# Weight ring numbered through the sections, second-block token-major evictions on ScalarE, and three moved steps, in a two-block hybrid transformer kernel

## The reference

```python
def first_block(x, c, ...):            # two hybrid_layers, then rms_norm(h, final_g)
    mod = silu(c) @ w_ada + b_ada      # shift, scale, gate
    u = rms_norm(x, g) * (1 + scale) + shift
    z = u @ w_in                       # 18 pieces: q, k, v, gates of three attentions
    merged = (sigmoid(ma) * (ya @ w_br_a) + sigmoid(mb) * (yb @ w_br_b)
              + sigmoid(mc) * (yc @ w_br_c))
    return x + gate * (merged @ w_out)

def second_block(x, c, ctx, c_ctx, ...):   # two mixer_layers
    h  = x  * (1 + scale)   + shift        # latent tokens
    hc = cx * (1 + scale_c) + shift_c      # 256 context tokens
    a_q, a_i, a_ff, a_fb, b_q, b_k, b_v, c_q, c_k, c_v, d_q, d_k, d_v, g = split(h @ w_in)
    # ... and the same pieces of hc @ w_in
    y_a = hgrn2_mixer(...)       # gated scan in both directions, rms-normed per head
    y_b = global_gqa(...)        # latent queries on latent + context keys
    y_c = diff_attention(...)    # softmax(q1 k1) - lam * softmax(q2 k2)
    y_d = window_gqa_latent(...) # window with a sink
    x_new = layer_norm(alpha * x + gate * (concat(y_a..y_d) * silu(g) @ w_out), ln_g, ln_b)
    # the first layer also makes cx_new in the same way; the last does not
```

## Time and profile before

| | |
|---|---|
| median of 3 runs | 1502.31 us (1502.21 to 1502.62) |
| profiled execution, its own time | 1501.21 us |
| span of its instructions | 1499.2 us |
| mean granted TensorE clock | 0.987 |
| TensorE busy | 96% of the span |
| VectorE / ScalarE / GpSimd busy | 37% / 27% / 10% |
| DMA engines, mean share | 40%, 147 GB/s |

### The profile page before, as it was taken

The page is one execution under the profiler, slowest core; times in us unless marked ns, Lnnn a source line. Parts: engine busy times, 40 slices in busy tenths (PEclk is TensorE's granted clock), DMA queues, the critical chain, the costliest instruction groups (busy, mean ns, idle before and its releaser), DMA issues.

```text
span 1499.2 us, 20302 instructions
## 1 busy us (share of the span) xinstructions
PE 1440.3 (96%) x8186; PEld 1169.1 (78%) x8186; DVE 550.4 (37%) x1295; ACT 408.1 (27%) x755; POOL 146.2 (10%) x191
## 2 busy tenths in 40 slices
PE   5999999999999999999999999999999998999986
PEld 3888788888878878888888888876777787877765
DVE  1252212112126332314244422145663631455454
ACT  1112212412021222333312313232342412433332
POOL 0110200000011030000111100012220000142100
PEclk9999999999999999999999999999999999999999
DMA  9544544355445444443333433345315342322200
GB/s 375 219 158 152 202 169 169 144 193 206 159 169 197 168 169 169 150 175 134 123 137 113 140 113 113 140 168 204 129 62 196 113 155 84 141 85 85 85 28 29
DMA packets 31484, 221.95 MB, mean 148 GB/s; under 512 B 3872, under 2 KB 4000, under 8 KB 4896
## 3 DMA queue, kind: packets, MB, share of 16 engines
q1 hardware_dynamic: 31392, 220.67, 40.0%
HBM read 219.60 MB, written 1.05 MB: 147 GB/s over the span
## 4 chain that ended last, share of the span: by engine, by line
PE 90%; DVE 4%; ACT 2%; DMA 1%; issue 1%; POOL 1%; SPq 0%; DVEq 0%; ACTq 0%; POOLq 0%
PE event L869 45%; PE event L860 9%; PE event L1029 6%; PE event L1073 5%; PE logits L961 3%; PE mixed_out L1017 3%; PE event L826 3%; PE turns L980 3%; PE event L1041 2%; PE event L1100 2%; DMA ring<-in_w 1%; PE event L1173 1%; PE event L891 1%; PE event L1054 1%; PE event L848 1%
## 5 line engine op out<-in xcount | busy, mean ns | idle before, releaser
L869 PE MATMUL event<-u,ring 128*128 128x256 f32 x3200 | 718.7, 383 | 12.0 <-DMA ring<-in_w 4.9
L869 PEld LDWEIGHTS event<-u,ring 128*128 128x128 f32 x3200 | 605.4, 191 | 112.8 <-issue 22.7
L860 PE MATMUL event<-ring,u 128*128 128x256 f32 (+1 forms) x704 | 151.0, 371 | 0.0
L860 PEld LDWEIGHTS event<-ring,u 128*128 128x128 f32 x704 | 127.3, 190 | 22.1 <-issue 6.2
L1248 ACT ACTIVATE region<-event 128x512 f32<-128x512 f32 x72 | 43.1, 598 | 292.1 <-PE event L869 291.8
L1284 ACT ACTIVATE S<-logits,stat 128x512 f32<-128x512 f32 (+2 forms) x160 | 84.0, 535 | 130.2 <-DVE stat L1628 125.5
L1976 POOL TENSOR_TENSOR raw<-raw,tables 128x512 f32<-128x512 f32 (+1 forms) x28 | 33.6, 1201 | 772.3 <-PE event L891 464.6
L1073 PE MATMUL event<-region,ring 128*128 128x256 f32 x384 | 85.3, 380 | 2.9 <-DVE region L1771 2.9
L1029 PE MATMUL event<-region,ring 128*128 128x256 f32 x384 | 84.4, 380 | 0.0
L1073 PEld LDWEIGHTS event<-region,ring 128*128 128x128 f32 x384 | 72.2, 190 | 15.7 <-issue 6.4
L1029 PEld LDWEIGHTS event<-region,ring 128*128 128x128 f32 x384 | 72.6, 190 | 11.1 <-issue 1.4
(11 more groups left out here) (206 smaller groups left out, 1318.0 us busy)
## 6 DMA issues: line engine op xcount, KB each, us to landing
ring<-in_w SPq DMA_DIRECT2D x204, 1024.0 KB, 4.8
tables<-in_two SPq DMA_DIRECT2D x1, 1600.0 KB, 9.0
x<-in_x SPq DMA_DIRECT2D x1, 1024.0 KB, 15.1
x<-in_ctx SPq DMA_DIRECT2D x1, 1024.0 KB, 7.0
out<-x SPq DMA_DIRECT2D x4, 256.0 KB, 2.1
tables<-in_one SPq DMA_DIRECT2D x1, 832.0 KB, 10.9
tables<-in_late SPq DMA_DIRECT2D x1, 512.0 KB, 7.0
consts<-in_common SPq DMA_DIRECT2D x1, 320.0 KB, 3.4
```

The costliest lines, as they stand in the source:

```text
L860: ins = mm(bank[:, t * 256:t * 256 + width], mem.u[:, q, k, t * P:(t + 1) * P], wt[:, k * 256:k * 256 + width], start=k == 0, stop=k == KB ...
L869: ins = mm(bank[:, j * 256:(j + 1) * 256], wt[:, k * 256 + j * P:k * 256 + j * P + P], mem.u[:, q, k, :], start=k == 0, stop=k == KB - 1)
```

## The change

1. Ring slots are numbered by the row of the unit in the whole weight array, not in the section. Each used-up unit requests the row five further on, over the ends of sections as well.
2. In the second block's projections ScalarE evicts `vv`, `hi` and `fv` (both the latent's and the context's, in `one1` too). VectorE keeps `av`, `bv`, `cv` of the first block.
3. `feed 1 v1` in `two0` moves from in front of `fv` to behind `hi`.
4. `feed 0 v1` at the end of `two0` moves in front of the second half of `kk 1`, so on ScalarE its biases come ahead of the eviction of `kk 1`.
5. `norm h0` in `two1` moves to the front of its slot, ahead of the second half of `fv 1`.

```diff
-                      proj("fq"), ("rot", "fk", 0), ("mod", "v1"), ("feed", 1, "v1"), proj("fv"), ("rot", "fq", 0), proj("hi"), proj("ff", 1),
+                      proj("fq"), ("rot", "fk", 0), ("mod", "v1"), proj("fv"), ("rot", "fq", 0), proj("hi"), ("feed", 1, "v1"), proj("ff", 1),
...
-    return s + [("mean", 0), ("half", proj("kk", 1)), ("var", 0), proj("kk", 1), ("feed", 0, "v1")]
+    return s + [("mean", 0), ("half", proj("kk", 1)), ("var", 0), ("feed", 0, "v1"), proj("kk", 1)]
...
+    n = next(h for h, items in enumerate(fill) if ("norm", "h0") in items)
+    fill[n].remove(("norm", "h0"))
+    fill[n].insert(0, ("norm", "h0"))
...
-            n = u + RING if u + RING < len(units) else len(units) + u % RING
-            if row + n < ROWS:
+            n = row + u + RING
+            if n < ROWS:
...
-                slot = u % RING
-                eng.dma_start(mem.ring[:, slot, :], dram["w"][row + n]).then_inc(sems[f"landed{slot}"], 16)
+                slot = n % RING
+                eng.dma_start(mem.ring[:, slot, :], dram["w"][n]).then_inc(sems[f"landed{slot}"], 16)
...
-                slot = u % RING
+                row = first_row(sec) + u
+                slot = row % RING
...
-                    eng.wait_ge(sems[f"landed{slot}"], w.at(f"landed{slot}", 16 * (u // RING + 1)))
+                    eng.wait_ge(sems[f"landed{slot}"], 16 * (row // RING + 1))
...
-                if name in ("av", "bv", "cv", "hi", "fv", "vv"):
+                if name in ("av", "bv", "cv"):
                     continue
...
+                if name == "vv":
+                    both = split2(bank)
+                    act(to["gv"], both[:, :, 0:P], func)
+                    act(to["nv"], both[:, :, P:2 * P], func).then_inc(drained[e % BANKS], 1)
+                elif name in ("hi", "fv"):
+                    act(to[name], split2(bank), func).then_inc(drained[e % BANKS], 1)
...
-            elif kind == "proj" and item[1] in ("av", "bv", "cv", "hi", "fv", "vv"):
+            elif kind == "proj" and item[1] in ("av", "bv", "cv"):
```

More of the change, by code:

```diff
@@ L341, in __init__ @@
         events = sum(self.events(i) for i in script)
-        units = sum(map(has_unit, script))
         for b in range(BANKS):
             n[f"full{b}"] = n[f"drained{b}"] = len(range(b, events, BANKS))
-        for s in range(RING):
-            n[f"landed{s}"] = 16 * len(range(s, units, RING))
         for q in ("logits_ready", "exps_done", "probs_ready", "turned", "turns_copied", "mixed", "y_copied"):
@@ L691, in program @@
                      lambda n, s: ctx.enter_context(nc.psum_tensor(n, s, F32)))
-        names = sorted({q for sec in SECTIONS for q in sec.per}) + [
+        names = sorted({q for sec in SECTIONS for q in sec.per}) + [f"landed{s}" for s in range(RING)] + [
             "pe_links", "dve_links", "act_links", "pool_links", "consts_in", "cond_in", "x0_in", "params_in", "rest_in", "tables_in", "stored",
@@ L1233, in body @@
                     func = ACT.Silu
-                if name == "kk" and q == 0:
+                if name == "vv":
[4 more added lines that the diff above has]
+                    act(to[name], split2(bank), func).then_inc(drained[e % BANKS], 1)
+                elif name == "kk" and q == 0:
                     eng.wait_ge(sems["rope_done"], w.at("rope_done", 0))
@@ L1572, in body @@
                     dst, src = mem.one["bv"][:, :, 0:132], src[:, :, 0:132]
-                elif one:
+                else:
                     dst = mem.one[name][:, :, i * 256:(i + 1) * 256]
[L1575 to L1581, removed]
                 eng.tensor_copy(dst, src).then_inc(drained[e % BANKS], 1)
```

## The result

The changed kernel takes 1493.74 us (median of 5 runs, 1492.07 to 1495.74); the kernel before took 1502.21 us (5 runs) beside it. The ratio is 0.9945, 95% interval 0.993 to 0.9959: 8.5 us faster. The forecast was 1490.7 us, 11.65 us faster.

The account below looks back on a forecast made before the run. TensorE, busy 96% of the span, was taken as the bound, so only its waits and slow clock could be won. 4.8 + 3.5 + 4.3 - 0.95 = 11.65 us gave 1490.7 us; own range 1489.8 to 1493, 8 in 10 1488 to 1497.

Parts of the forecast that it names:

- the three places: End of `two0`, scan of `two0`, ahead of first `outa` of `two1`; clock falling at two would make the forecast wrong.
- The other sign: At `ff 1` in the scan of `two0`: starting less than 3 us earlier than before would make the forecast wrong.
- a rival's 1494.2: At `ff 1`: `hi`'s eviction and the biases hold it up by all that was won; 1494.2 us, chance 0.12.
- Ring and bias: End of `two0`: the 4.88 us wait for weights goes, a 2.2 us gap stays; 4.8 us won, bounds 2.7 and 5.5.
- The open cost, the clock: End of `two0`: whether the 2.8 us of slow clock behind the gap come back too.
- The row against it: Start of `one1`: behind a 2.36 us gap two units took 15.90 us instead of some 14.3, up to 1.9 lost.
- Context's scalings: Scan of `two0`: without the scalings ahead, the 4.92 us gap becomes 2.7; 3.5 us won, bounds 2.3 and 4.1.
- the cap that the prediction worked out at `ff 1`: VectorE's maxima of job 7, ahead of `ff 1`, end about 4.1 us earlier, so the scan wins at most 4.1 us.
- Scan norm: Ahead of first `outa` of `two1`: gap goes from 3.60 to 1.4 us, clock holds; 4.3 us won, bounds 1.5 and 4.3.
- `vv`: Start of `two0`: `silu 1` waits behind `vv` on ScalarE, gates start 3.15 us later; 0.95 us lost, bounds 0 and 1.
- The rival in which the clock falls at every remaining gap: At every gap that stays the clock falls for as long as before; 5.55 us won, 1496.8 us, chance 0.15.
- The rule by the gap's length: All remaining gaps are below its limit, so the clock holds everywhere; 12.95 us won, 1489.4 us, chance 0.15.

## Why the prediction was right, and where it was off

The order of events was right at all four places; the sum was 3 us too large, and nearly all of that is the clock. By its own signs the forecast did less well than by its number. It was to be called wrong if the clock fell at two of the three places, and it did fall at two: the scan and the end of `two0`. The other sign, `ff 1` less than 3 us earlier, did not show, but barely: `ff 1` begins at 1106.20 instead of 1107.58, which is 3.04 us earlier once this trace's late start (1.66 us) is taken off. The time lies in the range for 8 in 10 (1488 to 1497), above the forecast's own range (1489.8 to 1493), and nearest to a rival's 1494.2, in which edit 3 brings nothing; that is chance, since edit 3 brought 4.2 us.

- **Ring and bias (4.8; measured 3.74).** The gap was 2.33 us against 2.2. The open cost, the clock, was set at 0.7 us by the gap of 2.13 that had held; it was 1.7. This is the mis-sized term. The row against it had been read too high and set aside: 15.90 - 14.3 is 1.6 us, not 1.9, and at full clock the same 64 records took 14.76 us (four traces), so that fall cost 1.1. I had also costed edits 1 and 4 as one and never against edit 1 alone. Worked out, the eviction ahead of the biases would have given a shorter gap. Edit 1 brings 6.3 us (5.9 by the second trace of the kernel before), and edit 4 takes 2.6 back.
- **Context's scalings (3.5; measured 3.71).** The gap was 2.53 against 2.7, and the clock fell. That it cost nearly nothing is explained by the cap that the prediction worked out at `ff 1` (at most 4.1): with the clock at full the stage gave 3.94. One step of the working has no reason: its terms give 1084.8 for the end of the maxima, and 1084.2 was taken. It was the right one (1086.47 in the new trace, less the offset of 2.33, is 1084.14); with 1084.8 the gap would have been forecast at about 3.3 us.
- **Scan norm (4.3; measured 3.96, edit 5's share 3.9).** The gap was 1.38 against 1.4, and the clock held. `mix` waited 0.84 us where 0.7 was forecast.
- **`vv` (-0.95; measured -0.95).** The gates start at 958.05, 3.2 us later than in the earlier trace rows once the offset of 1.38 is taken off. Not forecast: 0.3 us won in `one1`, where a wait of TensorE for ScalarE's squares went from 1.83 to 1.55 us in every version in which ScalarE evicts `hi` and `fv`.
- **The unchanged last gap (0; measured -1.67).** No rival had this. The clock fell here in both traces of the changed kernel and in none of the other twelve; so the clock at a place can differ between versions that do not touch it. What in the changed kernel brought it about is not shown.

By the trace: 10.74 - 1.67 = 9.1 us. The rest up to the medians' 8.5 lies inside what the same kernel shows from one execution to the next. That the first trace of before held the worse clock of the two (1.28 us worse than its repeat) made every clock term worked out from it a little too large.

The rival in which the clock falls at every remaining gap came true at three places of four (the scan, the end of `two0` and the last gap; ahead of `outa` it held), but not "for as long as before": behind gaps of 2.3 to 2.5 us it was low for about 3 us of work, behind the long ones (3.6 to 6.5 us) mostly until 5 to 6 us after TensorE had started again. The rule by the gap's length, by which none of these gaps would cost anything, would have given 1489.4 us. The Trainium skill states it in "TensorE: Matmul & The Clock Gate", section "HAM oscillation — how this bites in real kernels"; these traces do not agree with it: behind the gap of 2.33 us the clock fell in five traces of five.

## What to carry to other kernels

Cost each edit of a bundle alone as well as with the others: here one edit took back 2.6 us of its neighbour's 6.3, and another lost 2.2 us by its trace alone (1.5 by the medians), and beside the rest between 0.35 won and 1.3 lost. When a long stall goes, look at which instruction releases TensorE next, and put that one first in its queue. A short gap can be worth more than its length (0.9 us of it cost 2.6 here), or nothing, where the next wait is set by another engine (the scan and `ff 1`).

## What the runs showed of the hardware

In the 14 traces the clock behind TensorE's idle gaps of 1.24 us and more, from `one1` on, went as follows.

| gap | place | fell in |
|---|---|---|
| 3.6 to 6.5 us | the three long ones | 17 of 17 |
| 2.43 | `ff 1`, edit 3 alone | 1 of 1 |
| 2.35 | start of `one1` | 10 of 14 |
| 2.33 | end of `two0` | 5 of 5 |
| 2.3 to 2.5 | scan | 5 of 8 |
| 2.12 | last | 2 of 14 |
| 1.80 | ahead of `outb` | 0 of 14 |
| 1.44 | end of `two0` | 0 of 4 |
| 1.37 | ahead of `outa` | 2 of 6 |
| 1.24 to 1.83 | five further places | 0 of 34 |

Longer gaps fell oftener, but the length alone does not decide: 2.12 us held in 12 traces and 1.37 us fell in two. Two traces of the same version agreed at every gap but one (start of `one1`, kernel before: fell once, held once), while versions differed at the same gap. What in a version decides was not found. Two traces are also few: the mean granted clock of the changed kernel's five executions runs from 0.990 to 0.994, where 3 us at half clock make 0.001, so the clock did not fall alike in all of them.

Also unexpected is what the 128x2 operations of VectorE show. Counted over the rows of all 14 timelines in which one stands alone: of its TENSOR_SCALAR and TENSOR_TENSOR instructions, the 126 that began while an instruction of POOL was under way took 0.30 to 1.25 us, and every one ended 0.00 to 0.03 us behind POOL's. The 714 others took 0.16 to 0.23 us. RECIPROCAL of the same size took 0.17 us in all 42 cases beside POOL. So POOL's instruction holds up the first two kinds to its end, even for two columns, and the third not at all. In the scan this put 1.07 us on TensorE's path without edit 2 and again with edit 3 alone; with `fv` evicted by ScalarE it did not come up there.
